# Attention heads of two kinds in one woven order, with value products per tile from a ring of four

## The reference, cut to what matters

```python
def diff_attend(q, k, v, lam):
    s = jnp.einsum('bhqd,bhkd->bhqk', q, k).astype(jnp.float32)
    p = jax.nn.softmax(s, axis=-1).reshape(b, h2 // 2, 2, nq, k.shape[2])
    w = p[:, :, 0] - lam * p[:, :, 1]
    return jnp.einsum('bhqk,bhkd->bhqd', w.astype(v.dtype), v)
...
    ql = axial_rope(ql, n) * scale
    kl = axial_rope(kl, n)
...
    s = jnp.concatenate([s_loc.reshape(b, NA_HEADS, rows, GRID_W, n_loc), s_ctx], axis=-1)
    p = jax.nn.softmax(s, axis=-1)
    o = jnp.einsum('bhrqjk,bhrjkd->bhrqd', p_loc, vb) + jnp.einsum('bhrqc,bhcd->bhrqd', p_ctx, vc)
```

## Time and profile before

| what | value |
|---|---|
| time, median of 3 runs | 3038.77 us (3030.85 to 3039.6) |
| the profiled execution | 3050.23 us, of which the span from first to last instruction is 3048.5 us |
| PE, PEld busy | 94%, 77% of the span |
| DVE, ACT, POOL busy | 56%, 28%, 10% |
| granted TensorE clock, mean | 0.959 of full speed |
| mixer of the first layer | from 798 to 1047 us of the span |
| mixer of the second layer | from 2430 to 2613 us |

### The profile page before, as it was taken

One profiled execution on the slowest core, in us unless ns is written; L12 is line 12 of the kernel. 1 busy time (PEld: TensorE's weight loads), 2 busy tenths in 40 slices (PEclk: granted clock), 3 DMA queues, 4 the chain that ended last, 5 costly groups with the idle time before them and its releaser, 6 DMA issues.

```text
span 3048.5 us, 39841 instructions
## 1 busy us (share of the span) xinstructions
PE 2874.7 (94%) x14770; PEld 2340.1 (77%) x14770; DVE 1718.3 (56%) x2840; ACT 856.6 (28%) x1147; POOL 292.2 (10%) x279
## 2 busy tenths in 40 slices
PE   6999999999779999999999899999998979999998
PEld 5888888877543578888888788888876744678887
DVE  7676676669673356766676772222247664443334
ACT  3221122141363332211221422112232264432222
POOL 1000000024322110000000100000004232000000
PEclk8999999999877999999999999999998979999999
DMA  5333333321220013333333232111212220123232
GB/s 201 117 117 124 111 117 139 103 77 55 56 59 7 21 49 117 117 122 107 123 118 117 76 110 70 62 55 63 74 50 84 74 66 7 55 81 101 91 99 84
DMA packets 63374, 264.94 MB, mean 87 GB/s; under 512 B 8880, under 2 KB 11824, under 8 KB 53680
## 3 DMA queue, kind: packets, MB, share of 16 engines
q1 hardware_dynamic: 50608, 180.17, 18.0%
q0 software_dynamic: 11520, 75.11, 7.6%
q10 hardware_dynamic: 1152, 8.39, 0.7%
HBM read 252.89 MB, written 2.10 MB: 84 GB/s over the span
## 4 chain that ended last, share of the span: by engine, by line
PE 83%; DVE 10%; ACT 4%; issue 2%; DMA 1%; POOL 0%; ACTq 0%; SPq 0%; DVEq 0%
PE ps L1431 74%; PE ps L1670 2%; DVE conv_acc L1184 2%; PE ps L1597 2%; PE ps L1625 1%; PE ps L1605 1%; DVE w_lo L934 1%; DVE rstd L987 1%; DVE nmax L1289 1%; ACT e_sb L846 1%; DMA x<-in_xT 1%; ACT probs_t L860 1%; DVE mod_start_acc L1366 1%; DVE y_hi L1023 0%; DVE sq L1011 0%
## 5 line engine op out<-in xcount | busy, mean ns | idle before, releaser
L1431 PE MATMUL ps<-y_hi,w_hi 128*128 128x512 f32 (+1 forms) x3184 | 912.5, 350 | 65.3 <-DVE y_lo L1015 31.2
L1431 PE MATMUL ps<-y_lo,w_hi 128*128 128x512 f32 (+1 forms) x3184 | 907.8, 349 | 0.0
L1431 PE MATMUL ps<-y_hi,w_lo 128*128 128x512 f32 (+1 forms) x3184 | 900.6, 346 | 0.0
L1431 PEld LDWEIGHTS ps<-y_hi,w_hi 128*128 128x128 f32 x3184 | 519.9, 191 | 164.5 <-issue 35.8
L626 ACT ACTIVATE w_hi<-w_raw 128x1024 fp32r<-128x1024 f32 (+1 forms) x290 | 326.6, 1128 | 1063.9 <-PE ps L1431 1063.9
L1431 PEld LDWEIGHTS ps<-y_lo,w_hi 128*128 128x128 f32 x3184 | 517.1, 190 | 75.9
L1431 PEld LDWEIGHTS ps<-y_hi,w_lo 128*128 128x128 f32 x3184 | 515.0, 190 | 77.7 <-issue 0.2
L934 DVE TENSOR_TENSOR w_lo<-w_raw,w_hi 128x1024 fp32r<-128x1024 f32 (+1 forms) x290 | 384.8, 1327 | 322.3 <-ACT w_hi L626 320.0
L949 DVE SCALAR_TENSOR_TENSOR mod_acc<-mod_raw,cact,mod_acc 128x256 f32<-128x256 f32 x896 | 360.2, 479 | 0.0
L1431 PE MATMUL ps<-h_lo,w_hi 128*128 128x512 f32 (+1 forms) x1254 | 356.8, 344 | 0.0
L1431 PE MATMUL ps<-h_hi,w_hi 128*128 128x512 f32 (+1 forms) x1254 | 356.3, 344 | 0.0
(11 more groups left out here) (162 smaller groups left out, 2033.8 us busy)
## 6 DMA issues: line engine op xcount, KB each, us to landing
w_raw<-in_w_up SPq DMA_DIRECT2D x176, 512.0 KB, 3.5
mod_raw<-in_w_mod POOLq DMA_DIRECT2D x64, 1024.0 KB, 5.1
w_raw<-in_w_down SPq DMA_DIRECT2D x64, 704.0 KB, 4.1
w_raw<-in_w_in SPq DMA_DIRECT2D x36, 512.0 KB, 3.5
mod_start<-in_w_mod ACTq DMA_DIRECT2D x8, 1024.0 KB, 22.0
w_raw<-in_w_out SPq DMA_DIRECT2D x16, 512.0 KB, 3.5
stack<-qk_hi SPq DMA_DIRECT2D x48, 96.0 KB, 2.1
band<-in_rpb POOLq DMA_DIRECT2D x16, 224.0 KB, 6.6
```

The lines of the kernel that those rows point to most:

```text
L1431: mm = pe.matmul(slot[s][:, at:at + b - a], w[s][:, k, :], r[:, k, a:b], start=(k == 0 and n == 0), stop=(k == kc - 1 and n == 2))
```

## The change

The attention steps get a new order. A diff head comes first. Then, for each further diff head, its six (in the second layer four) steps are laid in pairs between the steps of the near head before it: diff, diff, near, diff, diff, near. The last near head comes last. A diff head's context tiles stand between its latent ones. The value products are no longer done per head and 512 queries wide: each tile of 128 queries is multiplied by the values one step after its transposes, from a ring of four buffers (`ring`), into one of two PSUM places, and ACT copies the 64 by 128 result out at once.

Around it: mix_in's last three pairs of units change order (values, near k, near q); DVE rotates q at u = 9 and k at u = 11 and does fewer taps in those two (`TAPS`), so that the last tap moves from u = 13 to u = 15; ACT makes the first two `qk_hi` before it empties unit 14; POOL makes the first two `qk_lo` before it masks the bands; the bands of heads 0, 1 and 3 are loaded first and that of head 2 during the steps; the scaling of the near heads' q moves behind the mixer's value copies. The root of the convolution's variance, its inverse (in parts), the norm, the pooling and the pointwise products move from ahead of the steps into steps 0 to 7 (0 to 6 in the second layer).

```diff
 def attention_steps(with_ctx):
-    out = []
-    for h in range(HEADS):
-        tiles = [(t, False) for t in range(LAT // P)] + [(t, True) for t in range(CTX // P)] * with_ctx
-        out += [("diff", h, (t,), c, n == len(tiles) - 1) for n, (t, c) in enumerate(tiles)]
-    for h in range(HEADS):
-        tiles = [((0, 1), False), ((2, 3), False)] + [((0, 1), True)] * with_ctx
-        out += [("na", h, t, c, n == len(tiles) - 1) for n, (t, c) in enumerate(tiles)]
-    return out
...
+        return [lat[0], ctx[0], lat[1], lat[2], lat[3], ctx[1]]
...
+    out = diff(0)
+    for h in range(1, HEADS):
+        tiles = diff(h)
+        for n, step in enumerate(near(h - 1)):
+            out += tiles[2 * n:2 * n + 2] + [step]
+    return out + near(HEADS - 1)
...
+TAPS = (5, 6, 6, 6, 6, 6, 1, 6, 1, 6, 6, 6, 1)
...
-    probs_t = [place(f"probs_t{b}", [P, TOK // P, LAT], at=at) for b, at in enumerate((at_y, at_probs1))]
+    ring = [place(f"probs_t{b}", [P, TOK // P, P], at=at_y + (12 + b) * chunk) for b in range(4)]
...
+                def copy_probs(step):
+                    n = made[0]
+                    keys = CTX // P if step[3] else TOK // P
+                    t.wait("turned")
+                    if n >= 4:
+
+                        act.wait_ge(sems["pv"], n - 3)
+                    act.activation(ring[n % 4][:, 0:keys, :], turn[:, 0:keys * P].rearrange("p (k q) -> p k q", q=P),
+                                   ACT.Copy).then_inc(sems["probs_t"], 1)
+                    made[0] += 1
...
+                    t.wait("pv")
+                    act.activation(mixed[(4 if kind == "diff" else 6) + h // 2][rows, at:at + P],
+                                   outs[rows, 512 * (n % 2):512 * (n % 2) + P], ACT.Copy).then_inc(sems["tile_out"], 1)
...
+                    if k == 1:
+                        t.wait("conv_var")
+                        act.activation(rstd[:, 0:n], outs[:, 0:n], ACT.Sqrt, bias=eps_t[:, 1:2], scale=1.0 / W).then_inc(sems["conv_sqrt"], 1)
...
+                    if 1 <= k <= parts:
+                        if k == 1:
+                            t.wait("conv_sqrt")
+                        part = slice(CTX * (k - 1), CTX * k)
+                        dve.reciprocal(rstd[:, part], rstd[:, part]).then_inc(sems["conv_rstd"], 1)
...
+                def weigh_values(k):
+
+                    kind, h, tiles, ctx = steps[k]
+                    n_tile = made[1]
+                    pe.wait_ge(sems["probs_t"], n_tile + 1)
+                    if n_tile >= 2:
+
+                        pe.wait_ge(sems["tile_out"], n_tile - 1)
+                    rows = slice(DH * (h % 2), DH * (h % 2) + DH)
+                    col = (0 if kind == "diff" else W) + DH * h
+                    keys = range(LAT // P if ctx else 0, TOK // P)
+                    for n_key, key in enumerate(keys):
+                        mm = pe.matmul(outs[rows, 512 * (n_tile % 2):512 * (n_tile % 2) + P], v_sb[:, key, col:col + DH],
+                                       ring[n_tile % 4][:, n_key, :], start=(n_key == 0), stop=(key == TOK // P - 1))
+                    mm.then_inc(sems["pv"], 1)
+                    made[1] += 1
...
                     for s in range(2):
                         if k < len(steps):
                             scores(k, s)
                         if turned and s < len(turned[2]):
...
                             transpose_probs(k - 2, s)
-                            tiles_turned += 1
...
+                        if closed and s < len(closed[2]):
+                            weigh_values(k - 3)
+                    if k < WC:
+                        pool_product(k)
+                    if k - pointwise_at in range(WC):
+                        conv_pointwise(k - pointwise_at)
```

More of the change, by code:

```diff
@@ L371, in scores_before @@
         return sum(2 * len(attention_steps(n < LAYERS - 1)) for n in range(layer))
-    def diff_scores(layer):
-        return 2 * sum(s[0] == "diff" for s in attention_steps(layer < LAYERS - 1))
     def turned_before(layer):
@@ L451, in _ @@
                     stack_heads(p.layer)
+                if p.name == "mix_in":
+                    with loop(sp, 0, NA_Q // 2) as i:
+                        for s in range(2):
+                            fetch(p, i, s)
+                    for i in range(NA_Q // 2, p.pairs):
+                        for s in range(2):
+                            fetch(p, i, s)
+                    continue
                 start = 1 if p is PHASES[0] or p.name == "mix_out" else 0
@@ L559, in mixer @@
[L559 to L572 removed]
+                low_parts((1, 3))
@@ new lines, in mixer @@
+                steps = attention_steps(layer < LAYERS - 1)
+                for k, (kind, h, tiles, ctx) in enumerate(steps):
+                    if k == last_step(layer, "diff", 1):
+                        pool.wait_ge(sems["stacked1"], 16 * 12 * (2 * layer + 1))
+                        load_band(2)
+                    if k == last_step(layer, "diff", 1) + 3:
+                        t.wait("band_raw", 16 * 2)
+                        mask_band(2, 0)
+                    if k == last_step(layer, "diff", 1) + 4:
+                        mask_band(2, 1)
@@ L1345, in mixer @@
+                for first, c in norm_from.items():
+                    for j in range(parts):
+                        if first + j >= len(steps) + 3:
+                            if j == 0:
+                                t.wait("head_sqrt")
+                            head_norm(c, slice(CTX * j, CTX * j + CTX))
+                dve.wait_ge(sems["turned"], turned_before(layer + 1))
                 for m in range(DC):
                     t.wait("y_hi")
+                    if m == DC // 2:
+                        dve.wait_ge(sems["pv"], turned_before(layer + 1))
@@ L1590, in scores @@
                     band = kind == "na" and not ctx
+                    if band and tile == 0:
+                        if h == 0:
+                            t.wait("na_scaled")
+                        if h < 3:
+                            pe.wait_ge(sems["band_ready"], layer * HEADS + (3, 3, 4)[h])
                     for a, b in spans(TOK)[1 if ctx else 0:]:
@@ new lines, in mixer @@
+                for s in range(2):
+                    pe.wait_ge(sems[slot_free[s]], pairs_done)
+                turn_values(0)
+                turn_values(1)
+                pe.wait_ge(sems["conv_acc"], (layer + 1) * WC * CONV_K)
+                for (a, b), at in zip(spans(n), (CONV_LAT, CONV_CTX)):
+                    for c in range(WC):
+                        mm = pe.matmul(outs[:, a:b], ones[:, :], conv_acc[c][:, at], start=(c == 0), stop=(c == WC - 1))
+                mm.then_inc(sems["conv_mean"], 1)
@@ new lines, in mixer @@
+                for k in range(2, TOK // P):
+                    turn_values(k)
+                t.wait("conv_sq", WC)
+                for a, b in spans(n):
+                    for c in range(WC):
+                        mm = pe.matmul(outs[:, a:b], ones[:, :], e_sb[:, 2 + c, a:b], start=(c == 0), stop=(c == WC - 1))
+                mm.then_inc(sems["conv_var"], 1)
+                pe.wait_ge(sems["rope_done"], layer + 1)
+                pointwise_at = n // CTX + 3
+                norm_at = [last_step(layer, "diff", h) + 5 for h in (1, 3)]
```

433 lines of the change are left out of this document (188 added, 245 removed).

## The result

The changed kernel takes 3052.67 us (median of 6 runs, 3049.23 to 3068.45), the kernel before 3039.18 beside it: a ratio of 1.0055, 95% interval 1.0029 to 1.008. It is slower by 0.3 to 0.8 per cent; the medians differ by 13.5 us. The forecast was 3035, no net change; the range held the time, the direction was missed. Its median lay between 3039 and 3051 from one set of runs to the next, so kernels of different sets are compared by their ratios or by their mixers, not by their medians.

The account below looks back on a forecast made before the run. TensorE was taken as the bound in near heads, waiting in diff heads. Starts of -3 and +2, first layer's rest -14 and second's +11 gave -4 us on 3050.2, or about 3035 from the median; range 3004 to 3064.

Parts of the forecast that it names:

- The second layer's steady state: Woven diff, diff, near steps in the second mixer: 18.35 us for three, 1.4 more than now.
- the two waits: TensorE in each triple's second diff step: 1.5 us for VectorE's scaling of near tiles, 0.8 for ScalarE's copy.
- 142 forecast: Second layer from step 6 to the end: 12, 5 x 18.35, 4.5 and 34, against 131 now; loss 11.
- the 2456 laid out: Second layer's start: POOL's last tap, bands, masks and low parts end at 2456, holding up step 0's scaling.
- The value passes: Value products of 128 columns on TensorE: 0.137 us a pass, 1.65 a tile against 1.36 now.
- The start of the first layer: First scores at 811, POOL through at 819, step 8 at 860 against 863 now: -3 us.
- 170, so the end is at 1030: First mixer from step 8 on: 39, 2 x 46, 5 and 34 us, against 184 now; gain 14.
- 46, 51 and 73: First layer's terms by head: 46 a cycle, 46 with the norm's 5, and 39 with 34 for last near head and drain.
- the clock: Rival, both mixers: TensorE bound everywhere, so half clock costs everywhere; 25 us, so 3060; chance 0.24.
- 60 us more of half clock: Clock rival's case: 60 us more of both mixers at 0.50 costs 25; it decides from some 30 us on.
- fewer waits than laid out: Rival, woven steps: ScalarE and VectorE run ahead, three steps take 15.9 us; 35 us faster, 3000; chance 0.30.

Follow-up runs that it names:

- filler: Changed kernel plus six unread identity transposes on TensorE ahead of each transposing of a near tile in a diff step: 3051.44 us, ratio 1.0022 against the kernel before.
- masks_late: Changed kernel with GpSimd's six band masks moved behind the scalings of steps 0 to 5, low parts ahead of them: 3053.95 us, ratio 1.003 against the kernel before.

## Why the prediction missed

- **The second layer's steady state** was right: the two waits, where they stand, and 18.35 against 18.10 for three steps. The mixer was forecast 13 us longer and is 6.9. From its first near scores on it took 140 us (142 forecast). The start was priced too high: these scores come at 2473.9, not 2483, of which nearly 4 are mix_in's earlier end and the rest goes with GpSimd, whose first scaling came 9 us before the 2456 laid out.
- **The value passes** at 0.137 were priced too high by 0.016, which works for the change, 0.2 us a tile.
- **The start of the first layer** was right to 2 us in time (861.46 for 860), and GpSimd's first scaling too (819.6 for 819 to 821). For the scaling that was luck: the queue of masks and low parts was through sooner than laid out, and the first scores, with the factors made from them, came later.
- **The step that failed** is the sum of the first layer: "170, so the end is at 1030". It was laid out at full clock throughout. The mixer ended at 1048. From 861 on its clock was 0.91, a deficit of 17 us of 187, and the excess over the forecast lies where the deficit lies: 2, 7 and 8 us more than 46, 51 and 73, at clocks of 0.96, 0.88 and 0.89. The waits in it were laid out; what stays of half clock beside them was put at nothing. In *filler*, at 1.00, the same stretch takes 174 with 12 us of useless work in it, so 11 to 13 us are clock by that one profile (against 185 and 187 in the two of the changed kernel).
- **The rival "the clock"** was the nearest: half clock where TensorE is the bound, slower, with a chance of 0.24 and a price of 25 us. But its condition, 60 us more of half clock, did not come about. Both mixers together had 126 to 157 us of half clock in the three profiles before, and 89 and 96 in the two after. The better mix did hold the clock up; less half clock was left, and it cost more, because it had cost nearly nothing in diff steps, as the rival said, and the forecast counted on none in the rest.
- **The rival "fewer waits than laid out"** needed ScalarE to run ahead. It can't, in order behind an exponential. With that one copy moved both mixers are 22 us shorter (416.7 against 439.1), and with the products last too 36 (402.9). The rival had promised 35 below the forecast, though by waits alone, and a good part of the 22 is clock.
- **The baseline.** The loss of 8.7 in the mixers is against three profiles of before; the forecast subtracted from one whose first mixer, 250.1, was typical in two of three. That was no error. Of the median's 13.5 us, 5 aren't located.

## What to carry to other kernels

When tiles of another kind are woven into a pipeline, look at the shortest step that handles them, and at each in-order queue in it: what was one product, one transpose and one copy a step becomes two with a single place between them, and the order within the step must change with the order of the steps. The same edit (value products last) was worth 31 us in one order of steps and cost 9 to 23 in the other, by one profile each, so an order is judged only with its own best queues. And a forecast that leaves pauses of a us or two on TensorE should have a price for them as clock beside the one as waits: here it was 11 to 17 us in one layer and nothing in the other.

## What the runs showed of the hardware

Six transposes in each of 16 places, 0.75 us of useless work, went with a mean clock of 1.00 over 174 us where it had been 0.91 over 187. In the second layer waits of 1.23 and 0.74 us in each three steps went with 0.98. VectorE's products of 32 columns took 4.09 us for two while GpSimd worked on 128x896 masks, and 0.29 in the kernel before and in *masks_late*, where it didn't. And one program had a half-clock stretch of 30 us with TensorE busy 96 to 97% of it, in two of three executions, and a clock of 0.83 there in the third: its cause stays open.
